# Gate columns and narrow z pieces of a two-layer encoder trunk: three rounded passes in place of native float32

## The reference

```python
h = rms_norm(x, mix_pre_g[i])
z = h @ w_in[i]                      # one projection; its columns feed everything below
z_a, z_b, z_c, z_d, z_gate = split(z)            # 416, 512, 2304, 512 and 4 * 1024 columns
o_a, o_b, o_c, o_d = four attentions on z_a, z_b, z_c, z_d
gates = sigmoid(z_gate)              # (tokens, 4 branches, 1024)
merged = sum over n of gates[:, n] * (o_n @ w_branch[n])
x = x + rms_norm(merged @ w_out[i])
...                                  # layer 0: dense SwiGLU; layer 1: top-2-of-8 experts; then an input embedding
```

## Time and profile before

| | us |
|---|---|
| median of 3 runs | 2053.13 (2051.37 to 2054.71) |
| the profiled execution, its time | 2061.58 |
| its span, from first to last instruction | 2059.8 |

### The profile page before, as it was taken

The page is one execution under the profiler, slowest core; times in us unless marked ns, Lnnn a source line. Parts: engine busy times, 40 slices in busy tenths (PEclk is TensorE's granted clock), DMA queues, the critical chain, the costliest instruction groups (busy, mean ns, idle before and its releaser), DMA issues.

```text
span 2059.8 us, 26872 instructions
## 1 busy us (share of the span) xinstructions
PE 1968.7 (96%) x10030; PEld 1656.9 (80%) x10030; DVE 1344.1 (65%) x1486; ACT 1073.9 (52%) x1112; POOL 52.6 (3%) x104
## 2 busy tenths in 40 slices
PE   6999998999998999997899999999999999999986
PEld 5888887999986878886777888888788888888864
DVE  3345345555545434435678888888788888988864
ACT  4233334333325333233566776766677776777743
POOL 2100002000000100001000000000000000000000
PEclk9999999999999999998899999999999999999998
DMA  9533346555544633334698998999899999998970
GB/s 295 159 103 106 118 139 199 184 183 183 183 156 163 194 103 123 103 123 169 228 358 315 353 372 320 375 346 349 328 346 375 341 355 350 353 373 324 374 292 22
DMA packets 253439, 506.42 MB, mean 246 GB/s; under 512 B 8400, under 2 KB 90480, under 8 KB 253248
## 3 DMA queue, kind: packets, MB, share of 16 engines
q1 hardware_dynamic: 250656, 497.65, 68.2%
q0 software_dynamic: 2720, 7.91, 1.4%
HBM read 504.48 MB, written 1.05 MB: 245 GB/s over the span
## 4 chain that ended last, share of the span: by engine, by line
PE 85%; DVE 4%; DMA 4%; ACT 3%; issue 3%; POOL 0%; SPq 0%; DVEq 0%; ACTq 0%; POOLq 0%
PE ps L1042 25%; PE ps L984 17%; PE ps L1184 11%; PE ps L954 9%; PE ps L879 4%; PE ps L1127 4%; DMA ring<-in_moe_w_down_dram 3%; PE ps L857 3%; PE ps L1191 3%; PE ps L994 1%; PE ps L1003 1%; ACT down_hi_w L1387 1%; PE ps L1171 1%; PE ps L929 1%; PE ps L1023 1%
## 5 line engine op out<-in xcount | busy, mean ns | idle before, releaser
L1828 DVE TENSOR_TENSOR ring_lo<-ring,up_gate_hi_w 128x2048 fp32r<-128x2048 f32 x224 | 505.3, 2289 | 104.1 <-ACT up_gate_hi_w L1384 102.8
L1384 ACT CAST up_gate_hi_w<-ring 128x2048 fp32r<-128x2048 f32 x224 | 423.4, 1913 | 104.6 <-DMA ring<-in_moe_w_gate_dram 97.0
L1042 PE MATMUL ps<-up_gate_hi_w,tokens_hi 128*128 128x512 f32 x896 | 356.4, 398 | 1.2 <-DVE ring_lo L1828 1.2
L1042 PE MATMUL ps<-up_gate_hi_w,tokens_lo 128*128 128x512 f32 x896 | 350.7, 391 | 0.0
L1042 PE MATMUL ps<-ring_lo,tokens_hi 128*128 128x512 f32 x896 | 350.2, 391 | 0.0
L1833 DVE TENSOR_TENSOR down_lo_w<-ring,down_hi_w 128x2048 fp32r<-128x2048 f32 x112 | 256.1, 2287 | 27.9 <-ACT down_hi_w L1387 27.9
L1387 ACT CAST down_hi_w<-ring 128x2048 fp32r<-128x2048 f32 x112 | 214.4, 1915 | 56.4 <-DMA ring<-in_moe_w_down_dram 56.4
L1184 PE MATMUL ps<-hT,ring 128*128 128x256 f32 x1024 | 232.9, 380 | 0.0
L1184 PEld LDWEIGHTS ps<-hT,ring 128*128 128x128 f32 x1024 | 192.5, 190 | 27.8 <-issue 1.7
L1042 PEld LDWEIGHTS ps<-up_gate_hi_w,tokens_lo 128*128 128x128 f32 x896 | 168.9, 188 | 36.3
L1042 PEld LDWEIGHTS ps<-up_gate_hi_w,tokens_hi 128*128 128x128 f32 x896 | 169.0, 189 | 35.5 <-issue 1.6
(11 more groups left out here) (218 smaller groups left out, 2555.7 us busy)
## 6 DMA issues: line engine op xcount, KB each, us to landing
ring<-in_moe_w_gate_dram SPq DMA_DIRECT2D x112, 1024.0 KB, 5.2
ring<-in_moe_w_up_dram SPq DMA_DIRECT2D x112, 1024.0 KB, 5.2
ring<-in_moe_w_down_dram SPq DMA_DIRECT2D x112, 1024.0 KB, 8.8
ring<-in_w_in_dram SPq DMA_DIRECT2D x58, 1024.0 KB, 5.4
ring<-in_ffn_w_up_dram SPq DMA_DIRECT2D x16, 1024.0 KB, 5.4
ring<-in_ffn_w_gate_dram SPq DMA_DIRECT2D x16, 1024.0 KB, 8.0
ring<-in_ffn_w_down_dram SPq DMA_DIRECT2D x16, 1024.0 KB, 9.6
ring<-in_w_branch_dram SPq DMA_DIRECT2D x8, 1024.0 KB, 4.9
```

The costliest lines, as they stand in the source:

```text
L1042: m = mm(bank, xs[:, 4 * half + k, :], w[:, k, :], start=(half == k == n == 0), stop=(half == 1 and k == 3 and n == 2))
L1384: copy(up_gate_hi_w[:, j, :], ring[:, slot, :]).then_inc(run.up_gate_hi, 1)
L1828: v.tensor_tensor(ring_lo[:, slot, :], ring[:, slot, :], up_gate_hi_w[:, j, :], ALU.subtract)\
```

## The change

The gate columns and the narrow pieces become rounded products. The input is taken from `zT_hi` and `zT_lo`, which live on through the mixer (`zT_hi` now where `hT` is), and the four copies to `hT` go. Each of the 39 streamed products of a layer (`STREAM`: seven narrow pieces, 32 units) is split one step ahead: in the step before the one that uses it, ScalarE casts its weights to a high half (`stream_his`) and VectorE subtracts (`stream_los`), the low half into the ring slot. TensorE waits for `stream_split` ahead of the product. High halves alternate between two places each for units and (after the first) narrow pieces, and `qT`, `kz`, `lowT` and others are laid out anew to make room.

```diff
@@ memory
-        zT_hi = rounded("zT_hi", 11584, [P, NK, SEQ])
...
+        zT_hi = nc.alloc_sbuf_tensor_at("zT_hi", [P, NK, SEQ], F32R, offset=hT_at)
...
+        on_qa, on_heads, on_kc = [rounded(f"narrow_hi{at}", at, [P, NK, CW]) for at in (7488, 16448, 19520)]
+        NARROW_HI = [on_qa, on_kc, on_heads, on_kc, on_heads, on_kc, on_heads]
+        gate_hi_low = rounded("gate_hi_low", 12096, [P, NT, 4, P])[:, :, :, :]
+        gate_hi_b = rounded("gate_hi_b", 0, [P, NT, GATE0])[:, :, B0:C0].rearrange("p t (k c) -> p t k c", k=4)
@@ TensorE, narrow piece
-                            for t in range(NT):
-                                for k in range(NK):
-                                    m = mm(bank[:, t * SEQ:(t + 1) * SEQ], hT[:, k, t * P:(t + 1) * P], wv[:, k, :],
-                                           start=(k == 0), stop=(k == NK - 1))
+                            n = NARROW_Z.index(s[1])
+                            pe.wait_ge(stream_split, STREAM * layer + n + 1)
...
+                                    for i, (a, w) in product_parts((zT_hi, zT_lo), (hi, lo)):
+                                        m = mm(bank[:, t * SEQ:(t + 1) * SEQ], a[:, k, tile], w[:, k, :],
+                                               start=(k == i == 0), stop=(k == NK - 1 and i == 2))
@@ TensorE, unit
-                        loaded(pe, pos)
-                        wg = slot_of(pos).rearrange("p (k c) -> p k c", k=NK)
+                        pe.wait_ge(stream_split, STREAM * layer + len(NARROW_Z) + u + 1)
+                        hi, lo = gate_hi(u), stream_lo(layer, len(NARROW_Z) + u)
                         for k in range(NK):
-                            mm(bank[:, 0:SEQ], wg[:, k, (c % 2) * P:(c % 2 + 1) * P], hT[:, k, :],
-                               start=(k == 0), stop=(k == NK - 1))
+                            part = hi[:, k // 4, k % 4, :]
+                            for i, (w, a) in enumerate(((part, zT_hi), (part, zT_lo), (lo[:, k, :], zT_hi))):
+                                mm(bank[:, 0:SEQ], w, a[:, k, :], start=(k == i == 0), stop=(k == NK - 1 and i == 2))
@@ ScalarE
+            def stream_his(layer, n):
+                u = n - len(NARROW_Z)
+                if 2 < n < len(NARROW_Z):
+                    act.wait_ge(ex_ready, Z_DONE[(layer, NARROW_Z[n - 2][0])] + 1)
+                if u == 0:
+                    act.wait_ge(ex_ready, USE[(layer, "kva", NT - 1)] + 1)
+                if u == 1:
+                    act.wait_ge(pv_done, SETS * layer + SET0[4])
+                if u > 1:
+                    act.wait_ge(unit_ready, UNITS * layer + u - 1)
+                loaded(act, stream_slot(layer, n)[0])
+                if u < 0:
+                    copy(NARROW_HI[n][:, :, :], stream_full(layer, n)).then_inc(stream_hi, 1)
+                else:
+                    copy(gate_hi(u), quartered(stream_full(layer, n))).then_inc(stream_hi, 1)
...
-                for t in range(NT):
-                    for b in range(2):
-                        act.wait_ge(tile_split, tile_number(layer, "pre", t, b) + 1)
-                        copy(hT[:, 4 * b:4 * b + 4, t * P:(t + 1) * P], acc(t)[:, b, :].rearrange("p (i s) -> p i s", i=4))\
-                            .then_inc(pre_copied, 1)
...
+                            if i + 1 == len(WIDE_Z):
+                                stream_his(layer, 0)
...
+                            stream_his(layer, NARROW_Z.index(s[1]) + 1)
                             bank = taken(layer, "z", c, 0)
...
                         u = s[1]
+                        if u + 1 < UNITS:
+                            stream_his(layer, len(NARROW_Z) + u + 1)
                         act.wait_ge(unit_ready, UNITS * layer + u + 1)
@@ VectorE
+            def stream_los(layer, n):
+                u = n - len(NARROW_Z)
+                dve.wait_ge(stream_hi, STREAM * layer + n + 1)
...
+                    v.tensor_tensor(quartered(stream_lo(layer, n)), quartered(stream_full(layer, n)), gate_hi(u), ALU.subtract)\
+                        .then_inc(stream_split, 1)
...
+                    elif s[0] == "z":
+                        stream_los(layer, NARROW_Z.index(s[1]) + 1 if s[1] in NARROW_Z else 0)
...
+                        if u + 1 < UNITS:
+                            stream_los(layer, len(NARROW_Z) + u + 1)
                         dve.wait_ge(egate_done, n + 1)
```

More of the change, by code:

```diff
@@ L57 @@
 SLOT = 2048
-WORK = 26176
+WORK = 26432
 CW = SLOT // NK
@@ L382, in trunk @@
         xn = sb("xn", [P, NT, D_MODEL])
+        hT_at = place[0]
         hT = sb("hT", [P, NK, SEQ])
@@ L425, in trunk @@
         z = take(NT * GATE0).rearrange("p (t c) -> p t c", t=NT)
-        qT = take(8 * SEQ).rearrange("p (b s) -> p b s", b=8)
         qaT = take(4 * SEQ).rearrange("p (b s) -> p b s", b=4)
         kaT = take(4 * SEQ).rearrange("p (b s) -> p b s", b=4)
+        qT = take(2 * SEQ).rearrange("p (b s) -> p b s", b=2)
         probs = take(2 * NT * 2 * SEQ).rearrange("p (j t g s) -> p j t g s", j=2, t=NT, g=2)
-        take(NT * SEQ * 2)
+        lowT = take(4 * SEQ).rearrange("p (b s) -> p b s", b=4)
+        take(SEQ)
+        take(NK * SEQ)
+        oT = take(NK * SEQ)
+        post_tmp = oT.rearrange("p (t d) -> p t d", t=NT)
+        oT = oT.rearrange("p (b s) -> p b s", b=NK)
+        qcT = take(6 * SEQ).rearrange("p (b s) -> p b s", b=6)
+        kT = take(2 * SEQ).rearrange("p (b s) -> p b s", b=2)
+        kcT = take(8 * SEQ).rearrange("p (b s) -> p b s", b=8)
         NPT = 3
@@ L577, in loaded, with stream_slot, stream_lo, stream_full @@
             eng.wait_ge(slot_in[pos % RING], 16 * (pos // RING + 1))
+        def stream_slot(layer, n):
+            if n < len(NARROW_Z):
+                return WHERE[(layer, "z") + NARROW_Z[n] + (0,)], slice(0, CW)
+            order, c = divmod(n - len(NARROW_Z), 8)
+            return WHERE[(layer, "gate", BRANCH_ID[BRANCH_ORDER[order]], c // 2)], slice((c % 2) * P, (c % 2 + 1) * P)
+        def stream_lo(layer, n):
+            pos, columns = stream_slot(layer, n)
+            return ring_lo[:, pos % RING, :].rearrange("p (k c) -> p k c", k=NK)[:, :, columns]
+        def stream_full(layer, n):
+            pos, columns = stream_slot(layer, n)
+            return slot_of(pos).rearrange("p (k c) -> p k c", k=NK)[:, :, columns]
+        def gate_hi(u):
+            return gate_hi_b if u % 2 else gate_hi_low
+        def quartered(a):
+            return a.rearrange("p (t k) c -> p t k c", t=NT)
         def released(pos):
@@ L1092, in _ @@
                 turn_split_tile(layer, "pre", xn, 0)
-                narrow = False
                 for step_number, s in enumerate(MIXER):
@@ L1337, in swapped @@
                 elif item[-1] == "q":
-                    a = 0 if item[0] in "BD" else 2 + 2 * int(item[1])
+                    to = qT if item[0] in "BD" else qcT[:, 2 * int(item[1]):2 * int(item[1]) + 2, :]
                     bank = taken(layer, "swap", item, 0)
-                    copy(qT[:, a:a + 2, :], bank.rearrange("p (h s) -> p h s", h=2)).then_inc(ex_done, 1)
+                    copy(to[:, :, :], bank.rearrange("p (h s) -> p h s", h=2)).then_inc(ex_done, 1)
                 else:
@@ L1343, in swapped @@
                     n = 1 if item[0] in "BD" else 2
-                    a = 0 if item[0] in "BD" else 2 if item[1] == "0" else 4 + 2 * int(item[1])
+                    to, a = (kT, 0) if item[0] in "BD" else (kcT, 0 if item[1] == "0" else 2 + 2 * int(item[1]))
                     keys = bank[:, 0:n * SEQ].rearrange("p (h s) -> p h s", h=n)
-                    ins = copy(kz[:, a:a + n, :], keys)
-                    if a <= 2:
+                    ins = copy(to[:, a:a + n, :], keys)
+                    if a == 0:
                         for half in range(2):
                             r, other = slice(half * HD, (half + 1) * HD), slice((1 - half) * HD, (2 - half) * HD)
-                            ins = copy(kz[r, a + n:a + 2 * n, :], keys[other])
+                            ins = copy(to[r, n:2 * n, :], keys[other])
                     ins.then_inc(ex_done, 1)
```

31 lines of the change are left out of this document (13 added, 18 removed).

## The result

The changed kernel takes **2118.2 us** (median of four runs, 2114.1 to 2119.8) against 2052.3 before (2051.4 to 2054.7): ratio 1.0316, 95% interval 1.0297 to 1.0335. It is slower by 66 us; the forecast was 2119. The profiled execution took 2116.6 us, its span is 2114.8 (before 2061.6 and 2059.8).

What follows compares the result with a forecast made beforehand. TensorE was taken to bound the kernel. To the 2053.1 us median the prediction added 39 for waits net of cheaper products and 27 for the lower clock, giving 2119 us, range 2072 to 2140.

Steps and rivals of the forecast that it cites:

- waits and most drops: Main case: TensorE waits for VectorE's subtractions and most long waits lower the clock; 2105 to 2140 us, chance 0.57.
- The products: Gates and narrow pieces on TensorE: rounded passes of 120 ns save 26.5 us a layer, 53 for two.
- The waits: Ahead of second units, in the tail and around the second narrow piece: twelve waits of 2.4 us and more per layer.
- first head of C: Branch C's first head: softmax needs scores computed between its units; TensorE waits 5.2 us, a loss of 4.0.
- The sum without the clock: Mixer, net of cheaper products and waits: 19.6 us more per layer, 39 for both layers.
- the head without a rotation: One head per layer with no rotation ahead of the subtraction: gains in full, 1.0 us.
- The clock: Lower granted clock behind TensorE's long waits: 1.5 us each, 36 for all in both layers, three quarters taken, 27.
- six of six: Kernel before: all six TensorE waits of 2.0 us and more, at 2.4 GHz, were followed by a low-clock stretch.
- The clock holds: Rival: the waits come but the low clock seldom; 2092 us, up to 2105 with a few drops, chance 0.19.
- TensorE stays the bound: Rival: halves always ready in time, so the product saving shows; 2000 us; chance of any faster result 0.07.
- low half late only in branch C and the tail: Mixture rival: subtraction late only in those places; about 2030 us; chance of any faster result 0.07.
- The signs: Expected profile: 45 us of TensorE waits a layer, mixer clock 0.85 to 0.95, head transposes 12 to 13 us apart.

Runs made afterwards that it cites:

- products_alone: Changed kernel without casts and subtractions of the streamed weights; TensorE makes the same rounded passes from the split input, outputs not computed: 2005.5 us.
- start_order: Changed kernel with the first narrow piece's subtraction moved behind norm_b's sums of squares, where VectorE waits for GpSimd: 2118.0 us.
- waits_filled: Changed kernel with dummy TensorE passes put into the waits ahead of the gate products, the split no sooner: 2094.7 us.
- dve_order: Changed kernel with the subtraction for a head's second unit moved ahead of the rotation on VectorE, nothing else moved: 2081.9 us.
- all_three: both_early with the edits of tail_order and start_order added: 2018.4 us.
- both_early: Changed kernel with cast and subtraction of each head's second unit moved into its score step, the cast ahead of ScalarE's exponentials: 2035.1 us.
- start_pieces: start_order with the moved subtraction written as four instructions of 512 columns: 2116.3 us.
- tail_order: Changed kernel with cast and subtraction of the unit after next put ahead of the output weight's split in the tail: 2105.1 us.
- split_unwaited: products_alone with casts and subtractions of the same size made again on constants, TensorE not waiting for them: 2012.7 us.

## Why the prediction was right

The forecast was the mechanism "waits and most drops", 2119; measured 2118. The waits came as forecast; that the total agrees within 1 us is in part luck, as the points on the sum and on the clock show. By its steps:

- **The products.** 24 passes in 2.9 to 3.1 us, and 53 us less of TensorE: in products_alone its busy time falls by 53.8 us and the kernel's time by 47. The gate's passes have the forecast 120 ns (25 records in 3.10 us at clock 1.00). The 109 ns of the Trainium skill ("TensorE: Matmul & The Clock Gate", section "Back-to-back issue gap"), by which the forecast would have been 2095, do not show.
- **The waits.** Forecast and read from the changed kernel's timeline in layer 0: unit 1 3.7 and 3.62; then 2.7 and 2.69; 2.6 and 2.54; first head of D 4.3 and 4.20; first head of C 5.2 and 5.17; a later head of C 2.4 and 2.29; tail 2.5 and three times 2.39. The two heads with masks were put at 3.05 each and show 3.02 and 3.12. For example:

```profile
163.88 0.36 PE L1216 MATMUL ps<-zT_hi,gate_hi_b 128*128 128x256 f32 x1 [2.69 <-DVE ring_lo L1717]
...
249.10 0.55 PE L1216 MATMUL ps<-zT_hi,gate_hi_b 128*128 128x256 f32 x1 [5.17 <-DVE ring_lo L1717]
```

  The gate's subtraction was estimated at 1.22 us and takes that in VectorE's timeline; the chain counts 1.15 of it. At 247.82 us the chain of the first head of C reads as the prediction told it: end of the softmax, subtraction, gate.

```profile
246.94 0.88 DVE work L1847 x2
247.82 1.14 DVE ring_lo L1717
249.10 5.46 PE ps L1216 x24
```

- **The sum without the clock.** The start of the output product in layer 0 moved from 302.72 to 335.77, +33.05. The low clock took 13.7 of them (below), which leaves 19.35; the forecast was 19.6. By the distances between the transposes, less the low clock, the parts are near too: the first head of C costs 4.1 us (4.0 forecast), the first of D 3.2 (3.2), the three inside A 0.7, 1.8 and 1.6 (0.8, 1.7 and 1.6), the two with masks 2.1 and 2.2 (2.1 each). Two parts were off, and in part cancel: the head without a rotation gained 0.5 and not 1.0, and up to the first transposes behind unit 1 the kernel is 1.3 us ahead, not level. Of these, 1.1 us were there at the last wide subtraction (54.04 instead of 55.13), before any changed product; what brought them isn't shown.
- **The clock.** The sum was right, its making was not; that they meet is luck. Forecast: three quarters of twelve waits a layer, 1.5 us each, 13.5. Found in layer 0: seven stretches (six gates and the second narrow piece), 13.7 us, and in layer 1 eight. So fewer waits than nine were followed by the low clock in layer 0, and each cost more. The gates lose 1.3 to 2.7 us each, the most where the clock is low for the whole gate and into the next product (5.49 and 5.46 us instead of 3.11 at 136.80 and 249.10), and the narrow piece loses 2.6:

```profile
75.26 8.56 PE ps L1158 x48
...
85.11 5.95 PE ps L1158 x48
```

  The observation that all waits of 2.0 us and more are followed by a low clock did not hold: after 2.39 (three times), 2.69 and 3.12 us the gates of layer 0 ran at 1.00, while after 2.54 and 2.29 they did not. The count of six of six was wrong already: in the kernel before, the 2.1 us of products behind the wait of 2.52 us at 2004.29 ran at 1.00, so it was five of six at most. Nor does the length set the loss: in start_order the gate behind 3.63 us ran at full clock, in 3.13 us. waits_filled puts the price of the gates' stretches at 23 us; with the narrow pieces' share (8.56 and 7.26 us for 5.95, 4 us) the term was about 27.
- **The rivals.** "The clock holds", 2092, is what waits_filled makes of it by force: 2095. "TensorE stays the bound", 2000, is products_alone at 2005.5. The order that the prediction named as its condition, the subtraction ahead of the rotation, is dve_order, and it gave 2081.9: not enough. It took the place ahead of the exponentials (2035.1) and the new order in the tail (all_three, 2018.4) to come near. The mixture "low half late only in branch C and the tail" at 2030 is near both_early's 2035, where the tail alone was late.
- **The signs.** 38.5 us of waits a layer at the gates, 43.9 with the three around the second narrow piece (5.0, 3.3 and 2.5 in both layers), for 45 forecast. Clock 0.95 and 0.93 in the two stretches of layer 0's mixer, for 0.85 to 0.95. Transposes 12.7 us apart at the head shown, for 12 to 13; with a low clock or at the first head of a branch it is more, up to 18.9.
- **What was off and stayed hidden.** The sum was made against the profiled execution, 2128, and that came out at 2116.6: both mixers together are 66.7 us longer (the second output product starts at 1003.96 instead of 937.29; forecast 66), but what stands behind them was 11.7 us shorter in the profile of after than in that of before. Of this, 8.2 us are TensorE's waits for VectorE in the experts (L1003, now L1036): 13.9 us in the profile of before and 5.7 in that of after, at places that the change does not touch. The profile of before lay 9 us above its own median; against the medians, the error goes.

## What to carry to other kernels

A cheaper product that needs a prepared operand is worth what the order of the preparing engine lets through: walk that engine's queue from the event that frees it to the new instruction, at every kind of place where it occurs, and compare with the time at which the bound engine gets there. Here the same instructions gave +66 us or -40 us, by their place alone, and the good place for most of them was where the preparing engine itself waited for another (the exponentials). When a bound engine is made to wait for a few microseconds again and again, count the clock as a second cost, and don't expect a small gain ahead of such waits to reach the end.

## What the runs showed of the hardware that I had not expected

- Whether the granted clock falls behind a wait of 2.3 to 3.6 us isn't settled by its length: 2.39 us was followed by 1.00 in the changed kernel and by 0.58 over 4 us in start_pieces, at the same gate. The same gate behind 2.69 and 2.70 us took 3.11 us in the changed kernel and 5.46 in tail_order, which edits nothing there. What else decides it stays open.
- Dummy passes in the waits kept the clock up: 500 of them took it from 0.93 to 1.00 over the units of layer 0 and made the kernel 23 us faster.
- A GpSimd instruction of 0.19 us took 2.16 us beside one VectorE subtraction of 2.28 us and ended with it, and 0.56 us where the subtraction came in four pieces. GpSimd's next one, over the same 12 columns, took 2.30 us alone and 2.62 beside three of these pieces.
- The casts and some 51 us a layer more of busy VectorE (1446.8 us in split_unwaited, 1344.4 in products_alone) cost 7 us where TensorE doesn't wait for them.
